# A large fused transformer, state-space and convolution kernel: the square root of each norm issued ahead of two weight roundings

## The reference

```python
def _rms_norm(x, g):
    xf = x.astype(jnp.float32)
    y = xf * lax.rsqrt(jnp.mean(xf * xf, axis=-1, keepdims=True) + NORM_EPS)
    return (y * g.astype(jnp.float32)).astype(x.dtype)
...
        h = _rms_norm(x, norm_mix[l]) * (1.0 + sc1) + sh1
        ...
        x = x + g1 * (y @ w_out[l])
        h = _rms_norm(x, norm_ffn[l]) * (1.0 + sc2) + sh2
        x = x + g2 * _swiglu(h, ffn_gate[l], ffn_up[l], ffn_down[l])
...
def swiglu_ffn(u, w_gate, w_up, w_down):
    return (jax.nn.silu(u @ w_gate) * (u @ w_up)) @ w_down
```

## Time and profile before

| | |
|---|---|
| median of 3 runs | 3396.25 us (3395.53, 3396.25, 3400.5) |
| the profiled execution | 3395.65 us, its span 3393.9 us |
| mean granted TensorE clock | 0.887 of full speed |
| TensorE busy | 2895.9 us, 85% of the span |
| VectorE busy | 1336.2 us, 39% |
| GpSimd busy | 1267.9 us, 37% |
| ScalarE busy | 983.6 us, 29% |
| DMA | 264.47 MB, 78 GB/s mean |

### The profile page before, as it was taken

The page is one execution under the profiler, slowest core; times in us unless marked ns, Lnnn a source line. Parts: engine busy times, 40 slices in busy tenths (PEclk is TensorE's granted clock), DMA queues, the critical chain, the costliest instruction groups (busy, mean ns, idle before and its releaser), DMA issues.

```text
span 3393.9 us, 33284 instructions
## 1 busy us (share of the span) xinstructions
PE 2895.9 (85%) x12679; PEld 2312.3 (68%) x12679; DVE 1336.2 (39%) x1816; ACT 983.6 (29%) x1532; POOL 1267.9 (37%) x574
## 2 busy tenths in 40 slices
PE   4766569899999778999989976599999977799998
PEld 3645347688787556887878974477887754478876
DVE  6559863232203763222025225503221199532211
ACT  2112232233323453332223322223332211333321
POOL 1211659234443102444423445333444333134442
PEclk7777665899999998999989987799999988899999
DMA  7421223223323101223222210022332211023321
GB/s 218 152 84 62 72 90 112 70 79 99 96 83 82 38 26 50 80 93 96 90 64 87 88 63 1 0 75 75 99 99 84 78 62 37 25 75 99 95 82 59
DMA packets 271419, 264.47 MB, mean 78 GB/s; under 512 B 20844, under 2 KB 270285, under 8 KB 271309
## 3 DMA queue, kind: packets, MB, share of 16 engines
q1 hardware_dynamic: 271309, 262.96, 24.7%
HBM read 260.85 MB, written 2.10 MB: 77 GB/s over the span
## 4 chain that ended last, share of the span: by engine, by line
PE 72%; DVE 20%; issue 3%; ACT 2%; POOL 2%; SPq 0%; DMA 0%; DVEq 0%; POOLq 0%; ACTq 0%
PE bank L1008 18%; PE bank L1009 18%; PE bank L1010 18%; DVE v_cm L1924 5%; DVE ada_acc L2097 2%; PE bank L1060 2%; PE bank L1047 1%; PE bank L1049 1%; PE bank L1048 1%; PE bank L1083 1%; PE bank L1032 1%; PE bank L1326 1%; PE bank L1033 1%; DVE root L2030 1%; PE bank L1034 1%
## 5 line engine op out<-in xcount | busy, mean ns | idle before, releaser
L698 POOL TENSOR_TENSOR w_lo<-w_raw,w_hi 128x1024 fp32r<-128x1024 f32 (+1 forms) x408 | 968.0, 2385 | 1873.3 <-ACT w_hi L1532 1311.2
L1008 PE MATMUL bank<-h_hi,w_hi 128*128 128x512 f32 x1888 | 752.0, 398 | 91.9 <-DVE u_pad L1931 30.3
L1009 PE MATMUL bank<-h_lo,w_hi 128*128 128x512 f32 x1888 | 745.1, 395 | 0.0
L1010 PE MATMUL bank<-h_hi,w_lo 128*128 128x512 f32 x1888 | 744.2, 394 | 0.0
L1008 PEld LDWEIGHTS bank<-h_hi,w_hi 128*128 128x128 f32 x1888 | 361.0, 191 | 176.3 <-issue 69.3
L1532 ACT ACTIVATE w_hi<-w_raw 128x1024 fp32r<-128x1024 f32 (+1 forms) x232 | 232.4, 1013 | 646.8 <-PE bank L1010 624.0
L1009 PEld LDWEIGHTS bank<-h_lo,w_hi 128*128 128x128 f32 x1888 | 361.3, 191 | 76.1 <-issue 1.7
L1010 PEld LDWEIGHTS bank<-h_hi,w_lo 128*128 128x128 f32 x1888 | 360.8, 191 | 76.6
L2124 DVE TENSOR_TENSOR tmp<-sq,bank 128x512 f32<-128x512 f32 x88 | 60.6, 689 | 699.8 <-PE bank L1010 699.8
L1008 PE MATMUL bank<-a_hi,w_hi 128*128 128x512 f32 x704 | 282.6, 401 | 21.6 <-DVE a_lo L2128 21.6
L1009 PE MATMUL bank<-a_lo,w_hi 128*128 128x512 f32 x704 | 276.8, 393 | 0.0
(11 more groups left out here) (307 smaller groups left out, 3954.1 us busy)
## 6 DMA issues: line engine op xcount, KB each, us to landing
ada_w<-in_ada_w_dram SPq DMA_DIRECT2D x48, 512.0 KB, 6.4
w_raw<-in_ffn_gate_dram SPq DMA_DIRECT2D x22, 1024.0 KB, 5.3
w_raw<-in_ffn_up_dram SPq DMA_DIRECT2D x22, 1024.0 KB, 5.3
w_raw<-in_ffn_w_gate_dram SPq DMA_DIRECT2D x22, 1024.0 KB, 5.3
w_raw<-in_ffn_w_up_dram SPq DMA_DIRECT2D x22, 1024.0 KB, 5.3
w_raw<-in_ssm_w_in_dram SPq DMA_DIRECT2D x20, 1024.0 KB, 5.2
w_raw<-in_ada_w_dram SPq DMA_DIRECT2D x16, 1024.0 KB, 5.1
w_raw<-in_ffn_down_dram SPq DMA_DIRECT2D x16, 1024.0 KB, 5.2
```

The source lines that it names most:

```text
L698: pool.tensor_tensor(w_lo[parity][:, 0:nk, half], w_raw[parity][:, 0:nk, half], w_hi[parity][:, 0:nk, half].bitcast(F32), ALU.subtract).th ...
L1008: pe.matmul(dst[m][:], hi, src_hi(k0 + k), start=first and k == 0, stop=False)
L1009: pe.matmul(dst[m][:], hi, src_lo(k0 + k), start=False, stop=False)
L1010: ins = pe.matmul(dst[m][:], lo, src_hi(k0 + k), start=False, stop=last and k == nk - 1)
```

## The change

The last two roundings of a stage leave `round_and_square` and are issued in `norm`, behind the root. It is the same number of instructions on every engine, with the same operands and the same semaphores.

```diff
-                        for q in range(2):
-                            round_half(base + j + 2, q)
+                        if j < 4 * per_group - 1:
+                            for q in range(2):
+                                round_half(base + j + 2, q)
 
             def rms(name, z_last, width, eps):
...
             def norm(nn):
 
                 rms(f"n{nn}", SQ_BASE[f"n{nn}"] + DC - 1, D, NORM_EPS.get(nn, 1e-5))
+                if nn > 0:
+                    after = SLOT[ORDER[2 * nn]]
+                    for q in range(2):
+                        round_half(after + 1, q)
                 if nn == 8:
                     return
```

## The result

The changed kernel takes 3410.36 us (median of 6 runs, 3407.43 to 3413.71), the kernel before 3396.3 us (6 runs, 3394.58 to 3400.5). The ratio is 1.0036, with a 95% interval of 1.0026 to 1.0046: slower by 12.2 us (8.8 to 15.6). The two medians lie 14.1 us apart, which is inside that interval. The forecast was 10.5 slower, in a range of 3400 to 3411. The profiled execution took 3408.0 us, its span 3406.3 us, at a mean granted clock of 0.888.

What follows compares the result with a forecast made beforehand. TensorE, busy for most of the span, was seen standing still at seven norms behind a ScalarE and VectorE chain. Profiled 3395.65 us + 10.5 (7 x 1.5, net of the earlier root) = 3406.2; range 3400 to 3411.

Steps and rivals of the forecast that it cites:

- The root earlier, 0.58 per norm: At the seven norms n1 to n7, the root starts about 0.58 us earlier without two roundings in front.
- 4.0 us in the total: Gain from the earlier root over seven norms, 7 x 0.575, before the GpSimd overlap is counted.
- The roundings free on ScalarE: Behind the root, both roundings lie beside the reciprocal and cost ScalarE nothing; otherwise up to 1.99 us per norm.
- GpSimd pushed into the first scaling: At each norm GpSimd's second subtraction overlaps VectorE's first scaling by 2.25 us; 7 x 1.5 = 10.5 us lost net.
- Who is first hardly matters: At the scaling, GpSimd first costs +1.47 us per norm, VectorE first +1.53, both net of the earlier root.
- The port's price: VectorE's blocked work begins 0.2 us before GpSimd's record ends, by trace rows; the skill's 115 ns behind would give 12.5.
- The other things moved, nothing: Second `w_split` of a slot and SyncE's later load come 1.9 us later, covered by TensorE's products: cost nothing.
- The sum: Profiled execution 3395.65 us + 10.5 = 3406.2, or +0.31%.
- the bounds of 4 us for the clock: Allowance each side for TensorE's 1.2 GHz time after pauses, up to 1.5 us per norm: 3402 to 3410.
- TensorE makes up for it: Rival: full clock returns at the same moment despite later restarts, so half the shift is lost: +5.2, 3400.9; chance 0.07.

Runs made afterwards that it cites:

- the second experiment: Against the kernel before: root directly behind the squares, both roundings behind the norm's eight `h_hi`; 3396.61 us, ratio 1.0003.
- the second timing: Kernel with both roundings behind the eight `h_hi`, timed again against the kernel before: 3395.4 us, ratio 1.0003.
- the last experiment: The kernel before, unchanged, measured as if it were a changed one: 3396.51 us against 3395.46, ratio 1.0005.
- the fourth experiment: The change plus a tiny root between root and roundings, so VectorE's first scaling precedes GpSimd's second subtraction; 3410.35 us, ratio 1.0048 to the kernel before.

## Why the prediction was right

**The root earlier, 0.58 per norm: right at the norm.** It starts 1.16 us behind the start of the last sums (1.17 said), and the second experiment's pause of 6.97 gives 0.57 by itself. **4.0 us in the total: not shown.** The waits have it (-3.9) and two timings of the total do not. In the profile of the second timing TensorE is busy 2899.8 us, 3.9 more than before with the same instructions, at the same mean clock of 0.887. A profile of the first has 2905.1 at 0.885, and those of the change have 2894.2 and 2898.1, so TensorE's busy time differs by as much between runs of one kernel. Laying the record of the granted clock over TensorE's records tells what it is made of. TensorE is busy at 1.2 GHz for 482.5 us in the profile of before and 488.5 in that of the last experiment, for 502.3 and 489.9 with both roundings late, and for 478.6 and 486.4 with the change. Busy time less half of that is 2653.9 to 2656.2 us in all fourteen profiles. So the 3.9 us are work that fell into 1.2 GHz (half of 489.9 - 482.5 is 3.7), and the mean clock does not show them, because it counts the pauses too. Whether the early root brings this about is not shown: the four profiles with a late rounding at six or seven norms have 482.3 to 502.3, the two of the unchanged kernel 482.5 and 488.5. That cause stays open.

**The roundings free on ScalarE: right.** They lie from 1731.37 to 1733.36, and the first `h_hi` comes at 1737.71.

**GpSimd pushed into the first scaling: right, with its size.** The pair begins 0.99 us after the reciprocal does (1.0 said), the second subtraction 0.10 ahead of the scaling (0.09 said), the scaling takes 2.79 (2.8 to 3.0 said), and the pause at n4 is 9.01 (9.0 said). From the start of the reciprocal to TensorE's restart it was 6.21 to 6.27 us at the seven norms and is 8.25 to 8.32. That is 2.05 more, less 0.57 for the root: 1.48 per norm, against 1.47.

**Who is first hardly matters: right.** By the fourth experiment VectorE first costs 1.53 per norm (norm waits 72.4, 10.7 / 7), which is what was said.

**The port's price: the rows' figure holds.** Wherever a scaling waits for GpSimd here, its own work begins 0.20 us before the end of the other's record: 1734.79 + 2.34 = 1737.13 against 1734.89 + 2.79 - 0.75 = 1736.93. The 115 ns behind the end that the Trainium skill gives (page "SBUF — State Buffer", section "SBUF: two separate sides") would have made the sum 12.5. The Trainium skill took that figure from a DMA that waited for descriptors from GpSimd behind a VectorE copy, the other way round from here. The norm waits rose by 10.4, so the measurement decides against it; that the total of the change, 12.2, lies near 12.5 is due to the remainder, which the kernels without any such meeting show too.

**The other things moved, nothing: right** for the second slot. TensorE's waits by releaser name no `w_lo` at all, before or after the change or with both roundings late.

**The sum: 10.5 against 12.2 and 14.6.** The term of the norms measured 10.4, 0.1 from what was said. What the sum lacked is the remainder above, which the bounds of 4 us for the clock covered and the forecast set to nothing. The median of 3410.36 is inside the range, 0.64 us from its upper end. That it stayed inside is in part luck: the bounds were made for scatter at single norms, and what they took in is a remainder that no term of the sum stands for.

**TensorE makes up for it: refuted.** The rival wanted a shorter stretch at the low clock behind a later restart. Counted from TensorE's restart to the first 512-wide product recorded in under 0.5 us, in the profiles of before, of the change and of every experiment but the last, at the six norms where such products follow, it is 4.5 us on average behind 28 pauses of 9.0 to 9.1, 5.1 behind 13 of 7.5 to 7.6, and 4.5 behind 37 of 7.0 to 7.2. It is anything from 2.7 to 6.1, which is the scatter that the prediction's bounds allowed for. With that scatter the 0.6 between the first two is no clear difference, and it is well under the 1.5 that the rival needs. The total lost over twice the rival's 5.2.

## What to carry to other kernels

An instruction taken off a chain still has to run somewhere, and so does what follows it on other engines. Here ScalarE had 4 us of room beside the reciprocal, and the GpSimd work that each rounding releases had 0.22. Before moving a step, follow its results two engines on and lay their new times against everything that shares a resource with them; and where a total is too coarse for an edit of a few us, read the waits of the engine that bounds, which here told 0.1 us in every single profile. But such waits are not the total: the 3.9 us that the early root took out of them never showed in the time of the kernel.

## What the runs showed of the hardware

- VectorE and GpSimd take turns by whole instructions, even inside a run of back-to-back VectorE instructions: scalings of 0.75 and 2.83 us with a subtraction of 2.82 between them, at all seven norms of the fourth experiment. A meeting of 0.35 us cost 0.15 and one of 2.24 cost 2.05: in both the last 0.20 us of the other's record did not block.
- The RECIPROCAL of 128x512 in float32, SBUF to SBUF, is not part of this. It takes 3.345 to 3.353 us in the changed kernel too, with a 2.35 us subtraction beside it.
- The granted clock does not fall at once when TensorE stops. It fell 1.2 to 5.4 us into the pause at the seven norms of the fourteen profiles. In the changed kernel its pause at n4 begins at about 1730.74, and by stretches of 2 us (start:end, then us, then the busy times of PE, PEld, DVE, ACT and POOL, then the clock) it is:

```profile
1732.00:1734.00 2.00, 0.00 (x0) 0.00 (x0) 2.00 (x1) 1.35 (x2) 1.51 (x1) 1.00 0.00 0
1734.00:1736.00 2.00, 0.00 (x0) 0.00 (x0) 1.97 (x2) 0.00 (x0) 2.00 (x2) 0.61 0.00 0
1736.00:1738.00 2.00, 0.00 (x0) 0.00 (x0) 2.00 (x2) 0.28 (x1) 1.13 (x1) 0.50 0.00 0
```

It is still 2.4 GHz for the first 3.7 us or so, and 1.2 GHz from there on past the restart at 1739.75. Shortening this pause from 9.0 to 7.0 us takes away time at the low clock in which TensorE has nothing to do; on average it did not bring the full clock back sooner behind the restart (4.5 us in both).
- The mean granted clock of an execution is a poor measure of what the low clock costs. In the profile of before 765.2 us lie at 1.2 GHz, but TensorE is busy in only 482.5 of them; the other 282.7 are pauses. The part in which it is busy runs from 478.6 to 502.3 us over the fourteen profiles, and half of that difference, 12 us, is time, while their mean clocks lie between 0.884 and 0.888.
